# Layer norm with its means ahead of the squares and products of constants in its waits, and a GDN head whose root tables, decay, silu and cast stand elsewhere

## The reference

```
x <- LN(a*x + 0.5*FFN1(x)); x <- LN(a*x + Mixer(x)); x <- LN(a*x + 0.5*FFN2(x))
layer_norm: mu = mean(x); var = mean((x-mu)^2); (x-mu)*rsqrt(var+eps)*g + b
Mixer of layer 0: gated linear attention (GLA), 4 heads of 128 keys and 256 values
Mixer of layer 1: gated delta rule (GDN), 8 key heads with 2 value heads each:
  q, k, v = silu(causal conv of 4 taps); q, k scaled to length 1
  S_t = a_t (I - b_t k k^T) S_{t-1} + b_t k v^T ; o_t = S_t^T q_t   (in chunks, float32)
  o = rms_norm(o) * silu(z), then the output projection
Also returned: the new states of prompt and streams, and the last 3 conv inputs.
```

## Time and profile before

| | us |
|---|---|
| median of 3 runs | 3195.5 |
| the profiled execution | 3201.72 |
| its span | 3199.8 |
| PE busy | 3043.3 (95%) |
| DVE busy | 1328.1 (42%) |
| ACT busy | 1013.1 (32%) |
| POOL busy | 994.8 (31%) |
| mean granted clock of PE | 0.977 |

### The profile page before, as it was taken

How to read it: one execution, slowest core, us unless ns; L and a number is a source line. 1 busy time by engine, 2 the same in 40 slices (tenths; PEclk the granted TensorE clock), 3 DMA queues, 4 the chain that set the end, 5 groups by cost and what they waited for, 6 DMA issues and landing times.

```text
span 3199.8 us, 61556 instructions
## 1 busy us (share of the span) xinstructions
PE 3043.3 (95%) x25790; PEld 2904.8 (91%) x25790; DVE 1328.1 (42%) x1923; ACT 1013.1 (32%) x1751; POOL 994.8 (31%) x412
## 2 busy tenths in 40 slices
PE   8999999998999999999999989999999889999997
PEld 8999997887899999899999878888988778999997
DVE  3212253335521313621312666676376655312226
ACT  2111126333341111432111445444354434321112
POOL 3333343221433333433333411111211104333332
PEclk9999999999999999999999989999999979999998
DMA  3222221222122222122222111111111111222222
GB/s 132 73 77 80 74 82 51 81 75 83 60 73 74 79 79 77 64 74 77 73 86 73 63 45 62 62 69 63 67 62 69 63 43 53 79 73 79 80 73 78
DMA packets 62317, 230.60 MB, mean 72 GB/s; under 512 B 8257, under 2 KB 10177, under 8 KB 58754
## 3 DMA queue, kind: packets, MB, share of 16 engines
q1 hardware_dynamic: 56898, 200.27, 17.8%
q10 hardware_dynamic: 5184, 26.74, 2.2%
HBM read 209.76 MB, written 17.22 MB: 71 GB/s over the span
## 4 chain that ended last, share of the span: by engine, by line
PE 70%; issue 21%; POOL 4%; DVE 4%; ACT 1%; POOLq 0%; DVEq 0%; ACTq 0%
PE gem L228 60%; PE gem L559 4%; POOL wl L283 3%; POOL xl L509 1%; PE msc L420 1%; PE msc L435 1%; PE msc L726 1%; PE msc L734 1%; PE msc L544 0%; DVE work L497 0%; DVE work L925 0%; DVE work L928 0%; ACT small L1386 0%; PE msc L722 0%; DVE hh L961 0%
## 5 line engine op out<-in xcount | busy, mean ns | idle before, releaser
L283 POOL TENSOR_TENSOR wl<-raw,wh 128x1024 fp32r<-128x1024 f32 x368 | 931.9, 2533 | 2117.2 <-ACT wh L246 2117.2
L246 ACT CAST wh<-raw 128x1024 fp32r<-128x1024 f32 x368 | 386.5, 1050 | 1426.3 <-PE gem L228 1403.9
L228 PE MATMUL gem<-xh,wh 128*128 128x320 f32 x2688 | 612.6, 309 | 5.0 <-POOL wl L283 5.0
L228 PE MATMUL gem<-xl,wh 128*128 128x320 f32 x2688 | 612.5, 309 | 0.0
L228 PE MATMUL gem<-xh,wl 128*128 128x320 f32 x2688 | 612.4, 309 | 0.0
L228 PEld LDWEIGHTS gem<-xh,wh 128*128 128x128 f32 x2688 | 449.3, 188 | 5.9 <-ACT work L329 5.4
L228 PEld LDWEIGHTS gem<-xh,wl 128*128 128x128 f32 x2688 | 449.5, 188 | 0.0
L228 PEld LDWEIGHTS gem<-xl,wh 128*128 128x128 f32 x2688 | 449.3, 188 | 0.0
L350 DVE TENSOR_TENSOR work<-work,gem 128x640 f32<-128x640 f32 x88 | 72.3, 821 | 879.4 <-PE gem L228 843.4
L228 PE MATMUL gem<-hh,wh 128*128 128x320 f32 x1792 | 409.1, 310 | 2.1 <-issue 2.1
L228 PE MATMUL gem<-hl,wh 128*128 128x320 f32 x1792 | 408.9, 309 | 0.0
(11 more groups left out here) (266 smaller groups left out, 2924.3 us busy)
## 6 DMA issues: line engine op xcount, KB each, us to landing
raw<-wstream SPq DMA_DIRECT2D x368, 512.0 KB, 3.5
work<-gdn_s ACTq DMA_DIRECT2D x8, 1024.0 KB, 5.0
gdn_s_out<-work ACTq DMA_DIRECT2D x8, 1024.0 KB, 4.0
work<-gla_s ACTq DMA_DIRECT2D x4, 1024.0 KB, 6.9
gla_s_out<-work ACTq DMA_DIRECT2D x4, 1024.0 KB, 4.0
x<-x_in SPq DMA_DIRECT2D x2, 1280.0 KB, 8.1
y_out<-x SPq DMA_DIRECT2D x8, 320.0 KB, 2.2
gdn_p_out<-work ACTq DMA_DIRECT2D x8, 128.0 KB, 4.0
```

The lines of the kernel that those rows point to most:

```text
L228: mm = pe.matmul(gem[:, par, s, 0:HALF], w, r[:, k, s * HALF:(s + 1) * HALF], start=(k == 0 and n == 0), stop=(k == kts - 1 and n == 2))
L246: act.copy(wh[:, par, :], raw[:, par, :]).then_inc(hi_ready.sem, hi_ready.by)
L283: pool.tensor_tensor(wl[:, par, :], raw[:, par, :], wh[:, par, :].bitcast(F32), ALU.subtract)\
```

## The change

In the norm: the means' products end ahead of the squares' and have a signal of their own; DVE copies and squares the mean meanwhile, and takes the mean square straight from PSUM. PE multiplies a constant 13 times behind the means and 3 times behind the second and the third broadcast, into columns of `gem` that nothing reads. DVE begins to scale the first half before it builds the rest of the diagonals.

In the mixers: a root of a constant (`root_table`), whose result nothing reads, is issued where the root's table is to be loaded: in a GLA head after its second gate tile, in a GDN head at its start and again after `tile_out(3)`. In a GDN head the silu of the last conv tile moves from the fourth step to the head's end, the first decay of the streams from behind the steps into the fourth, and the cast that went with `tile_out(4)` ahead of its silu.

```diff
+        def idle_products(pe, n):
+            for _ in range(n):
+                pe.matmul(gem[:, 0, 0, HALF:HALF + 192], ident_r, cr[:].rearrange("p a n -> p (a n)")[:, 0:192],
+                          start=True, stop=True)
...
-            for a, src in ((0, zsum), (1, zsqs)):
-                pe.wait_ge(sum_ready.sem, sum_ready.at((KT - 1) * L + KT - 2, a))
-                means(a, src, True, False)
+            last = (KT - 1) * L + KT - 2
+            pe.wait_ge(sum_ready.sem, sum_ready.at(last, 0))
+            means(0, zsum, True, False)
             pe.wait_ge(evacuated[1].sem, evacuated[1].at(half(T)))
-            means(0, x[:, KT - 1, :], False, True)
+            mm = means(0, x[:, KT - 1, :], False, True)
+            mm.then_inc(mean_mm.sem, mean_mm.by)
+            pe.wait_ge(sum_ready.sem, sum_ready.at(last, 1))
+            means(1, zsqs, True, False)
             pe.wait_ge(sq_ready.sem, sq_ready.at(KT * L + KT - 1))
             mm = means(1, zsq, False, True)
             mm.then_inc(stat_mm.sem, stat_mm.by)
...
+            idle_products(pe, 13)
...
+                if j in (1, 2):
+                    idle_products(pe, 3)
...
-            dve.wait_ge(stat_mm.sem, stat_mm.at(L))
-            dve.tensor_copy(st[:, :, 0:TT], msc[:, 0, 0:16].rearrange("p (a t) -> p a t", a=2)[:, :, 0:TT])\
-               .then_inc(stat_step.sem, stat_step.by)
+            dve.wait_ge(mean_mm.sem, mean_mm.at(L))
+            dve.tensor_copy(st[:, 0, 0:TT], msc[:, 0, 0:TT]).then_inc(stat_step.sem, stat_step.by)
...
-            dve.tensor_tensor(tmp5, st[:, 1, 0:TT], tmp5, ALU.subtract).then_inc(stat_step.sem, stat_step.by)
+            dve.wait_ge(stat_mm.sem, stat_mm.at(L))
+            dve.tensor_tensor(tmp5, msc[:, 1, 0:TT], tmp5, ALU.subtract).then_inc(stat_step.sem, stat_step.by)
...
-            diagonal(diag_r, rstd, rest)
-            diagonal(diag_n, nmr, rest)
-            for s in range(2):
+            scale_half(0)
+            diagonal(diag_r, rstd, rest)
+            shift_half(0)
+            diagonal(diag_n, nmr, rest)
+            scale_half(1)
+            shift_half(1)
...
+        def root_table(act):
+            act.activation(small[:, 56:57], ones[:, 0:1], ACT.Sqrt)
...  act_gla, body
                 tile_out(1)
+                root_table(act)
                 for n in range(NCK):
...  act_gdn, body
+                root_table(act)
                 for j in range(2):
                     act.wait_ge(gdn["qk_mm"].sem, gdn["qk_mm"].at(s, j))
...
                 tile_out(3)
+                root_table(act)
...
-                    if t == 3:
-                        conv_end(3)
...
                 act.activation(d_ors, d_os, ACT.Sqrt).then_inc(gdn["ostd"].sem, gdn["ostd"].by)
-                tile_out(4)
+                act_split(act, gdn_tile(hf, i, 4, last), 0)
+                tile_out(4, split_done=True)
                 tile_out(5)
                 act.wait_ge(gdn["s_new"].sem, gdn["s_new"].at(s, 1))
                 act.dma_start(gdn_s_out[s], d_sin).then_inc(d_sst.sem, d_sst.by)
                 act.dma_start(gdn_p_out[s], d_s).then_inc(d_sst.sem, d_sst.by)
+                conv_end(3)
...  dve_gdn, body
                     if t == 3:
                         less_old(PT)
+                        decay_stream(0)
...
                 key_ends(PT)
-                decay_stream(0)
                 decay_stream(1)
```

More of the change, by code:

```diff
@@ L402, in build @@
         norm_a, norm_b = view(5 * TOK, 2, TOK), view(7 * TOK, 2, TOK)
+        mean_mm = Signal("ln_means_multiplied")
         stat_mm = Signal("ln_stats_multiplied")
@@ L419, in means @@
                 for t in range(TT):
-                    mm = pe.matmul(msc[:, 0, a * 8 + t:a * 8 + t + 1], src[:, t * P:(t + 1) * P],
-                                   cs[:, C_MEAN:C_MEAN + 1], start=first and a == t == 0, stop=last,
+                    mm = pe.matmul(msc[:, a, t:t + 1], src[:, t * P:(t + 1) * P],
+                                   cs[:, C_MEAN:C_MEAN + 1], start=first and t == 0, stop=last,
                                    skip_group_check=True)
                 return mm
-            for a, src in ((0, zsum), (1, zsqs)):
-                pe.wait_ge(sum_ready.sem, sum_ready.at((KT - 1) * L + KT - 2, a))
-                means(a, src, True, False)
+            last = (KT - 1) * L + KT - 2
+            pe.wait_ge(sum_ready.sem, sum_ready.at(last, 0))
+            means(0, zsum, True, False)
             pe.wait_ge(evacuated[1].sem, evacuated[1].at(half(T)))
-            means(0, x[:, KT - 1, :], False, True)
+            mm = means(0, x[:, KT - 1, :], False, True)
+            mm.then_inc(mean_mm.sem, mean_mm.by)
+            pe.wait_ge(sum_ready.sem, sum_ready.at(last, 1))
+            means(1, zsqs, True, False)
             pe.wait_ge(sq_ready.sem, sq_ready.at(KT * L + KT - 1))
@@ L431, in pe_ln @@
             mm.then_inc(stat_mm.sem, stat_mm.by)
+            pe.wait_ge(rounded.sem, rounded.at(0))
+            pe.wait_ge(evacuated[0].sem, evacuated[0].at(half(T)))
+            idle_products(pe, 13)
             for j, (b, dg, s) in enumerate(((0, diag_r, 0), (2, diag_n, 0), (0, diag_r, 1), (2, diag_n, 1))):
@@ L483, in dve_ln, with scale_half @@
             diagonal(diag_n, nmr, first)
-            diagonal(diag_r, rstd, rest)
-            diagonal(diag_n, nmr, rest)
-            for s in range(2):
+            def scale_half(s):
                 cols = slice(s * HALF, (s + 1) * HALF)
@@ L490, in dve_ln, with shift_half @@
                    .then_inc(scaled.sem, scaled.by)
+            def shift_half(s):
+                cols = slice(s * HALF, (s + 1) * HALF)
                 dve.wait_ge(scaled.sem, scaled.at(L, s))
@@ L1367, in conv_end, with tile_out @@
                         conv_out(j, s * 4 + (4 + j), freed)
-                def tile_out(j):
+                def tile_out(j, split_done=False):
                     T = gdn_tile(hf, i, j, last)
@@ L1378, in tile_out @@
                     act.activation(halves(d_z[j - 4]), slot(j % 2), ACT.Silu).then_inc(evacuated[j % 2].sem, evacuated[j % 2].by)
-                    act_split(act, T, j % 2)
+                    if not split_done:
+                        act_split(act, T, j % 2)
+                root_table(act)
                 for j in range(2):
```

## The result

The changed kernel takes **3204.98 us** in the median of 20 runs (3198.67 to 3216.74), the kernel before 3196.73 (3192.27 to 3205.71) in runs beside it: a ratio of 1.0021, 95% interval 1.0013 to 1.0028. Forecast was 3186.5, a gain of 9.0 us; the change loses 8.2, and the time lies outside the range.

The account below looks back on a forecast made before the run. PE was taken as the bound, busy 3043.3 of 3199.8 us. GDN heads -4.8, GLA 0 and norms -4.2 gave -9.0, subtracted from the median 3195.5 for 3186.5 us; own range 3181 to 3193.

Parts of the forecast that it names:

- Decay and silu moved: GDN head up to the streams' update: PE's wait for L1437 falls from 0.9 to 0.15-0.3 us, the update's to 0.3.
- Together -1.15 us at this point: GDN head at the streams' update: silu and first decay moved off the path start the update 1.15 us sooner.
- the GDN's -4.8: All GDN heads: five middle heads -4.0 us, head 3 -0.45, head 6 to 7 +0.25, head 7's end -0.6.
- POOL blocks the outputs' product: GDN head's end: the moved cast lets POOL block DVE's L1734 until +5.25 instead of +3.40 us; PE's 1.10 wait goes.
- The next head's start: Between GDN heads: scaled queries come 0.3 us sooner and PE's wait of 0.34 for them goes.
- Rival C, falls of the clock at the heads' ends: GDN heads' ends: PE's 3.5 us without dense products lowers the clock, at least 3.4 us a fall; six: 3207; chance 0.13.
- (A): GDN head's end: POOL does not block L1734, 13 us more gain, 3173.5 us; chance 0.14.
- (B): Norms: the clock holds through them, -10.5 us instead of -4.2, 3180 us; chance 0.13.
- D: Norms: at low clock they cost 3.6 us instead of winning, heads as forecast, 3194 us; chance 0.14.
- Norms: Six layer norms: -0.7 us each, -4.2 in all, bounds -10.5 and +3.6.
- half the interleaving's gain is lost: Norms at low clock: first broadcast starts 1.8 to 3.1 us behind the means instead of 1.93; -0.4 to +0.6 us.
- GLA: 0: GLA heads: the added root load and root on ACT are covered by its waits, 0 us; without cover +6.

Follow-up runs that it names:

- kernel 5: Changed kernel, second root kept, with a dummy silu on ACT ahead of the moved cast so POOL starts later; 3182.39 us, ratio 0.9961 to the kernel before.
- kernel 4: Changed kernel without the second root table, the one behind tile 3 of the GDN heads; 3178.47 us, ratio 0.9946 to the kernel before.
- kernel 2: Changed kernel with the norms of the kernel before, so only the mixers' changes remain; 3205.64 us, ratio 1.0026 to the kernel before.

## Why the prediction was wrong

It had the sign wrong. Its steps in turn:

- *Decay and silu moved.* Right: PE's wait for L1437 fell from 0.9 to under 0.2 and L1320's to 0.46 (0.3 forecast), and without the second root the way to the update is 1.15 us shorter (0.73 in the steps and 0.42 behind them). That the forecast's figure is met to the hundredth is luck.
- **The failed step: "Together -1.15 us at this point".** I counted the second root table as a load that goes from the head's end and never as one that comes behind tile 3. There load and root take 1.5 us of ACT ahead of the first new values, PE stands 0.72 us for these, and the steps lose 0.89 again, which kernel 5 still has and kernel 4 has not: -0.26 instead of -1.15 in each head, 7.1 us over eight (0.89 x 8). With it the GDN's -4.8 is +2.3; the head rows add up to some +3.8, since the seventh head loses 1.6 and the eighth 0.9 (forecast +0.25 and -0.6).
- *POOL blocks the outputs' product.* Right in mechanism and size: L1765 takes 3.31 us (predicted to end at +5.25 from the squares' end, so 3.3), 1.82 more to the outputs, and PE's wait for POOL behind them is gone but for one of 1.0 us (six before). The Trainium skill ("SBUF — State Buffer", "SBUF: two separate sides") states that of such a pair whoever starts first holds the port and the other blocks fully; both orders are here, 3.31 for DVE behind POOL and 3.11 for POOL behind DVE, and agree.
- *The next head's start.* Half right: the wait of 0.34 for the scaled queries is gone in six heads, but the squares come late enough to delay the copies of v, for which PE now stands up to 0.47 us (2.8 us in six heads), which I hadn't seen. So the 0.34 isn't won.
- *Rival C, falls of the clock at the heads' ends.* I gave it 0.13 as a whole story; it came as an addition: in the traces four of eight heads of the mixers alone have one, and two of after's. Each is 3.4 us long, half of the 6.8 from which I priced it. That the falls fill the gap between the +3.8 of the rows and the mixers' +8.8 is argued: the ways to the next q show 3.7 us of it in kernel 2, the rest lies elsewhere in the heads, and what a fall costs in the median run stays open. The other rivals are out: L1765 takes 3.31 us (A), the clock fell at all six norms (B), and the norms' interval ends below the +3.6 of D.
- *Norms.* Forecast -4.2; the medians of the norms alone are 1.5 below, the interval is -2.9 to +2.6. The products' length was inside my bounds (0.21 us from start to start at half clock, 0.11 at full). What failed is "half the interleaving's gain is lost": the traces show no gain of its own. That the low stretches shorten is right in half the norms of after (one of the others is longer, 10.2 us against 6.8), and may be what paid the later scale back.
- *GLA: 0.* Right as far as the traces go: 361.0 us between the norms in the mixers alone, 360.9 before. It wasn't tried alone.

Together: -9.0, and +7.1 for the root, +2.7 for the norms, leave +0.8, and the head rows add 1.5. The rest to +8.2, some 6 us, is not shown term by term; the falls at the heads' ends are the likeliest part of it.

## What to carry to other kernels

A table load is also a delay: before it is moved off a path, look at whose start it holds back, since here 1.28 us of load at the head's end were free and kept POOL behind DVE. For each added instruction name what is queued behind it at its new place as carefully as what is won at the old. As far as the norms' traces go, filling for PE pays when the engine that feeds the next step can do all its work meanwhile (5.97 us to the second tile's scale); placed between the pieces of that work it makes both wait (7.33).

## What was not expected of the hardware

An instruction of DVE that takes 1.49 us took 3.31 when POOL had begun 0.45 us ahead of it; POOL's took 3.11 instead of 2.38 when it began 0.63 behind. A shift of 1.1 us in one cast decided which, and with it 1.8 us a head. PE standing 2.3 us ahead of 1.28 us of transposes went with a fall of the granted clock to 0.50 in some heads and not in others of the same run.
